# A 16-expert stage on one core: the dense expert's down products by column halves at the end, all routed rows back through DRAM and PSUM, fifteen weight slots, a new order of places

## The reference

```
h2 = rms_norm(x, g)
for e in range(16):                      # combine: two of 16 weights per token are not zero
    he = silu(h2 @ w_gate[e]) * (h2 @ w_up[e])       # 1024 -> 512
    out = out + combine[..., e] * (he @ w_down[e])   # 512 -> 1024
x = x + out
x = x + sigmoid(x @ w_ple_gate) * (p @ w_ple_proj)
return rms_norm(x, final_g)
```

## Time and profile before

| | |
|---|---|
| time, median of 3 executions (lowest, highest) | 1636.68 us (1634.86, 1639.38) |
| profiled execution, its own time | 1639.89 us |
| span in its profile, granted clock of the core | 1638.1 us, 0.976 |
| PE, POOL, ACT, DVE busy over the span | 94%, 78%, 44%, 44% |
| expert stage | from about 1219 us to 1598 us of the span |

### The profile page before, as it was taken

One profiled execution on the slowest core, in us unless ns is written; L12 is line 12 of the kernel. 1 busy time (PEld: TensorE's weight loads), 2 busy tenths in 40 slices (PEclk: granted clock), 3 DMA queues, 4 the chain that ended last, 5 costly groups with the idle time before them and its releaser, 6 DMA issues.

```text
span 1638.1 us, 22007 instructions
## 1 busy us (share of the span) xinstructions
PE 1537.1 (94%) x7044; PEld 1167.6 (71%) x7044; DVE 712.8 (44%) x1316; ACT 720.8 (44%) x887; POOL 1270.2 (78%) x1513
## 2 busy tenths in 40 slices
PE   7999999999999989899999989999999898899966
PEld 5777877788877868688788867878775465476625
DVE  3986844301037968834101067174555221212225
ACT  4544543544446554444444435546332223245423
POOL 7997898999999996869999988977663335368823
PEclk9999999999999999999999999999999999999987
DMA  6754454667765543535676655645365989889980
GB/s 220 219 167 121 136 154 142 208 212 222 214 200 168 151 145 116 154 109 167 215 217 207 190 175 155 200 140 165 116 222 213 378 291 349 334 301 341 383 329 26
DMA packets 95429, 334.62 MB, mean 204 GB/s; under 512 B 11136, under 2 KB 15760, under 8 KB 94256
## 3 DMA queue, kind: packets, MB, share of 16 engines
q1 hardware_dynamic: 90752, 314.34, 58.5%
q10 hardware_dynamic: 3440, 14.93, 2.6%
q0 software_dynamic: 1152, 4.19, 0.7%
HBM read 323.17 MB, written 21.78 MB: 211 GB/s over the span
## 4 chain that ended last, share of the span: by engine, by line
POOL 52%; PE 26%; issue 15%; DMA 3%; DVE 2%; ACT 1%; SPq 1%; POOLq 1%; DVEq 0%; ACTq 0%
POOL w_lo L1835 52%; PE bank L684 7%; PE bank L1191 5%; PE bank L1245 4%; PE bank L1188 3%; PE bank L1211 3%; DMA arena<-in_experts 2%; PE bank L1260 1%; DMA outputs_by_expert<-xn 1%; PE bank L1284 1%; POOLq L1830 0%; DMA raw<-outputs_by_expert,tiny 0%; PE bank L713 0%; PE bank L1231 0%; PE bank L1086 0%
## 5 line engine op out<-in xcount | busy, mean ns | idle before, releaser
L1835 POOL TENSOR_TENSOR w_lo<-raw,w_hi 128x256 fp32r<-128x256 f32 x1416 | 1066.6, 792 | 140.4 <-ACT w_hi L1421 139.6
L684 PE MATMUL bank<-w_hi,hT 128*128 128x512 f32 x2240 | 714.6, 400 | 33.5 <-POOL w_lo L1835 13.4
L1421 ACT ACTIVATE w_hi<-raw 128x1024 fp32r<-128x1024 f32 x356 | 377.1, 1059 | 523.9 <-DMA raw<-in_stream 261.2
L684 PEld LDWEIGHTS bank<-w_hi,hT 128*128 128x128 f32 x2240 | 415.8, 191 | 136.7 <-POOL w_lo L1835 21.0
L684 PE MATMUL bank<-w_lo,hT 128*128 128x512 f32 x1120 | 441.5, 394 | 0.0
L1842 POOL TENSOR_TENSOR w_lo<-arena,w_hi 128x1024 fp32r<-128x1024 f32 x80 | 189.5, 2386 | 155.2 <-ACT w_hi L1421 154.8
L684 PEld LDWEIGHTS bank<-w_lo,hT 128*128 128x128 f32 x1120 | 213.2, 190 | 47.0
L1421 ACT ACTIVATE w_hi<-arena 128x1024 fp32r<-128x1024 f32 x80 | 84.3, 1056 | 104.1 <-PE bank L1191 40.7
L995 PE MATMUL bank<-w_hi,mixT 128*128 128x512 f32 x352 | 111.7, 399 | 5.4 <-DVE mixT L2254 5.2
L684 PE MATMUL bank<-w_hi,mixT 128*128 128x512 f32 x288 | 91.5, 399 | 3.9 <-POOL w_lo L1835 2.5
L2246 DVE SCALAR_TENSOR_TENSOR arena<-bank,tiny,arena 128x256 f32<-128x256 f32 x44 | 21.1, 484 | 158.6 <-ACT arena L1577 143.7
(11 more groups left out here) (389 smaller groups left out, 1901.1 us busy)
## 6 DMA issues: line engine op xcount, KB each, us to landing
raw<-in_stream SPq DMA_DIRECT2D x356, 512.0 KB, 3.6
arena<-in_experts SPq DMA_DIRECT2D x192, 512.0 KB, 7.2
rows_by_expert<-in_blank ACTq DMA_DIRECT2D x56, 128.0 KB, 3.2
arena<-in_stream SPq DMA_DIRECT2D x10, 512.0 KB, 12.2
gates<-rows_by_expert SPq DMA_DIRECT2D x3, 1024.0 KB, 7.3
outputs_by_expert<-xn SPq DMA_DIRECT2D x3, 1024.0 KB, 7.9
bias_skewed<-bias_windows SPq DMA_DIRECT2D x4, 512.0 KB, 5.2
outputs_by_expert<-in_blank ACTq DMA_DIRECT2D x4, 512.0 KB, 4.5
```

Source lines behind the costliest of these rows:

```text
L684: mm = pe.matmul(LIN[t][:, :], lhs[:, a, k0 + k, t * P:(t + 1) * P], w[:, k, :], start=(k0 + k == 0 and n == 0), stop=(k0 + k == nk - 1 an ...
L1421: act.activation(w_hi[:, s, :], src, ACT.Copy).then_inc(s_hi, 1)
L1835: part = nc.gpsimd.tensor_tensor(w_lo[:, i, c], raw[:, i, c], w_hi[:, i, c].bitcast(F32), ALU.subtract)
```

## The change

1. `RANKS` becomes (0, 13, 12, 1, 11, 10, 2, 9, 8, 3, 4, 5, 6, 7, 14): the wide place of each group of three comes first. Places 9 to 14 stay.
2. Fifteen slots: twelve in `arena` and the three buffers of `raw`, which the earlier part has done with.
3. The dense expert's four down quarters are no longer split and move from the start of the stage to its end, after the second projection quarter, in the order (g, n) = (0,0), (1,0), (0,1), (1,1). Its hidden values wait in `dense_he`.
4. The last place is stored (by ACT's queue) and gathered like the others; the spread, its matrix and the second set of addresses go.
5. Rows come back by column halves: first half of x first, and s_x is counted after each half.
6. ACT's program: in a paired place no `ahead` stands among the row splits, `needed` makes only the high parts of the place before, and `ahead` in `gated` reaches two quarters on.

```diff
-DEPTH = 12
+ARENA_SLOTS = 12
+DEPTH = ARENA_SLOTS + RING
-RANKS = (13, 12, 0, 11, 10, 1, 9, 8, 2, 3, 4, 5, 6, 7, 14)
+RANKS = (0, 13, 12, 1, 11, 10, 2, 9, 8, 3, 4, 5, 6, 7, 14)
+DENSE_DOWN = ((0, 0), (1, 0), (0, 1), (1, 1))
...
-    order = [("gu", -1, g, j) for g in range(2) for j in range(4)] + [("dn", -1, 0, n) for n in range(2)]
+    order = [("gu", -1, g, j) for g in range(2) for j in range(4)]
...
-    order += [("proj", 0)] + [("dn", POSITIONS - 1, g, n) for g, n in down_parts(POSITIONS - 1)] + [("proj", 1)]
+    order += [("proj", 0)] + [("dn", POSITIONS - 1, g, n) for g, n in down_parts(POSITIONS - 1)]
+    order += [("proj", 1)] + [("dn", -1, g, n) for g, n in DENSE_DOWN]
...
+                elif s >= ARENA_SLOTS:
+                    sp.wait_ge(s_hi, FRONT_Q)
+                    sp.wait_ge(s_lo, FRONT_Q)
...
+            def dense_down(g, n):
+
+                pe.wait_ge(s_td, ready[-1, g])
+                if (g, n) == DENSE_DOWN[0]:
+                    pe.wait_ge(s_flush, POSITIONS - 1)
+                elif g == 0:
+                    pe.wait_ge(s_flush, POSITIONS)
+                w = whole_quarter(down_at(-1, g, n))
+                for t in range(TT):
+                    for k in range(QK):
+                        mm = pe.matmul(AB[2 * t + n][:, :], dense_he[:, g, k, t * P:(t + 1) * P], w[:, k, :],
+                                       start=(g == 0 and k == 0), stop=(g == 1 and k == QK - 1), skip_group_check=True)
+                mm.then_inc(s_whole, 1)
...
-                rows_turned(0, 0)
                 pe.wait_ge(s_ad, ab.back(0))
-                expert_down(-1, 0, 0)
-                rows_turned(0, 1)
-                expert_down(-1, 0, 1)
-                rows_turned(0, 2)
-                rows_turned(0, 3)
+                for i in range(4):
+                    rows_turned(0, i)
...
-                last_spread()
+                for g, n in DENSE_DOWN:
+                    dense_down(g, n)
...
+            def needed(s):
+
+                for _ in range(split_before(s + 1) - hi.n):
+                    high()
...
-                ahead(last)
+                ahead(last, 2 if paired(p) else 6)
...
+                    if paired(p):
+                        hidden_split(p - 1)
+                        if p > 0 and not paired(p - 1):
+                            needed(down_at(p - 1, 1, 1))
+                        rows_split(p + 1, 0)
+                        rows_split(p + 1, 1)
                         rows_split(p + 1, 2)
                         rows_split(p + 1, 3)
                         gated(p, 1)
                         continue
...
+                        p, at = POSITIONS - 1, first_row(POSITIONS - 1)
+                        act.wait_ge(s_ycopy, POSITIONS)
+                        for h in range(2):
+                            act.dma_start(y_rows[at:at + rows_of(p), 512 * h:512 * h + 512],
+                                          staged(p)[64 * h:64 * h + rows_of(p), 0, 0:512]).then_inc(s_ystore[p % 2], 16)
+                ahead(GATE_AT - 1)
+                for i in range(4 * TT):
+                    h, c, t = i // 4, i // 2 % 2, i % 2
+                    if h == 0:
+                        act.wait_ge(s_back[c * TT + t], 16)
+                    act.wait_ge(s_added, max(1, i))
+                    w = tiny[:, 906 + 2 * c + t:907 + 2 * c + t]
+                    act.activation(AB[2 * (i % 2)][:, :], back[c * TT + t][:, h * 512:(h + 1) * 512], ACT.Copy,
+                                   scale=w).then_inc(s_weighed, 1)
...
+            def rows_back(h):
+
+                for i in range(4 * h, 4 * h + 4):
+                    t = i % 2
+                    dve.wait_ge(s_weighed, i + 1)
+                    v = x[:, t, h * 512:(h + 1) * 512]
+                    dve.tensor_tensor(v, AB[2 * t][:, :], v, ALU.add).then_inc(s_added, 1)
+                    dve.wait_ge(s_added, i + 2)
...
+                outputs_read(POSITIONS - 1)
+                dense_outputs(0)
+                dve.memset(tc(1006), 0.0).then_inc(s_added, 1)
+                rows_back(0)
+                dve.memset(tc(1006), 0.0).then_inc(s_x, 1)
+                rows_back(1)
+                dense_outputs(1)
+                dve.memset(tc(1006), 0.0).then_inc(s_x, 1)
```

More of the change, by code:

```diff
@@ L167, in is_whole @@
         return p < 0 or paired(p) or (tiles_of(p) == 1 and q[3] % 2 == 1)
-    return kind == "proj" or (kind == "dn" and paired(p))
+    return kind == "proj" or (kind == "dn" and (p < 0 or paired(p)))
 WHOLE = frozenset(s for s, q in enumerate(ORDER) if is_whole(q))
@@ L418, in program @@
         xf = [v[:].rearrange("p s w -> p (s w)")[:, 0:4 * P].rearrange("p (k t) -> p k t", k=4) for v in (wexp, prob)]
-        back = [raw[:, 0, :], raw[:, 1, :], raw[:, 2, :], logits[:].rearrange("p h w -> p (h w)")[:, 0:D]]
+        back = [gates[:, 1, t, :] for t in range(TT)] + [logits[:].rearrange("p h w -> p (h w)")[:, 2 * t * D:(2 * t + 1) * D] for t in range(TT)]
         order = tiny[:, 208:224].bitcast(mybir.dt.int32)
@@ L1730, in hidden_split @@
             def hidden_split(p):
-                if paired(p):
+                if p < 0 or paired(p):
                     tr.up()
@@ L1784, in experts_act @@
                         continue
+                    ahead(gate_up_at(p, 0, 0))
+                    hidden_split(p - 1)
+                    gated(p, 0)
+                    rows_split(p + 1, 0)
+                    ahead(down_at(p - 1, 1, 1) if p > 0 else gate_up_at(p, 0, 3))
+                    rows_split(p + 1, 1)
                     ahead(gate_up_at(p, 1, 0))
@@ L1793, in experts_act @@
                 for n in range(2):
-                    ahead(PROJ_AT[n])
                     act.wait_ge(s_lin, lin.up())
@@ L2517, in rows_rest, with dense_outputs @@
                                   e[:, 0, k:k + 2, 0:n].bitcast(F32), ALU.subtract).then_inc(s_td, 1)
+            def dense_outputs(n):
+                dve.wait_ge(s_whole, whole_before(down_at(-1, 1, n) + 1))
+                for t in range(TT):
+                    v = x[:, t, n * 512:(n + 1) * 512]
+                    own(dve.scalar_tensor_tensor(v, AB[2 * t + n][:, :], tc(292, t), v, ALU.mult, ALU.add))
+            def rows_back(h):
[5 more added lines that the diff above has]
+                    dve.wait_ge(s_added, i + 2)
             def outputs_read(p):
+                if p < 0:
+                    return
                 if paired(p):
@@ L2545, in outputs_read @@
                 dve.memset(tc(1007), 0.0).then_inc(s_flush, 1)
-            def last_weights():
-                for t in range(TT):
-                    dve.tensor_scalar(last_by_token[:, t, :], row_tab, last_rel[:, t:t + 1], w1[:, t, :], ALU.is_equal, ALU.mult)
-                    own(dve.tensor_scalar(last_part, row_tab, last_rel[:, TT + t:TT + t + 1], w2[:, t, :], ALU.is_equal, ALU.mult))
-                    i = dve.tensor_tensor(last_by_token[:, t, :], last_by_token[:, t, :], last_part, ALU.add)
-                    if t == 0:
-                        own(i)
-                i.then_inc(s_lastw, 1)
             def experts_dve():
```

142 lines of the change are left out of this document (37 added, 105 removed).

## The result

The kernel with the change takes 1623.42 us (median of 10 executions, 1615.94 to 1632.38). The kernel before took 1636.38 us on the same chip (median of 10, 1632.01 to 1644.47). The ratio is 0.9915, with a 95% interval of 0.9888 to 0.9942: 0.6 to 1.1% faster. The forecast was 1614 us, with a range of 1606 to 1630, so the time lies in the range, 9 us above the forecast.

The account below looks back on a forecast made before the run. PE and the DMA engines were taken as nearly used up by turns, with PE pausing at three holes and the end; 1639.9 profiled less 23.1 gave 1616.8, the median 3.2 lower, so 1614 us, range 1606 to 1630.

Parts of the forecast that it names:

- Dense products removed (10.9) and hidden at the end: Expert stage: two dense down blocks of 5.47 us leave PE's path, 10.9 us; at the end the gathers hide them.
- The three holes (16.6) and their slow restarts (8): PE's pauses where a wide place follows a paired one vanish with ACT's new order: 16.6 us, plus 8 us of restarts.
- The opening (7.9 and 2.5): Start of the routed places: PE waits for a wide place's rows, adding 7.9 us, and restarts slowly, adding 2.5.
- Two waits for `w_lo` (4.2): At wide places 3 and 6, behind paired ones, PE waits 2.1 us each for the first low part: 4.2 us added.
- Local shortage (1.5): Before the end of the routed places, weight loads fall short locally: 1.5 us added, between 0 and 12.
- The rival that loads are too slow: Stretches of paired places: SP's in-order waits use up the three-slot margin, costing 12 us instead of 1.5: 1624.5 us; chance 0.17.
- T': End of the last place's down products in the changed kernel, forecast at 1557.6 us against 1577.0 before.
- S: Time for the last place's store on ACT's queue to land at the stage's end, taken as 6 us.
- the late store: Rival at the stage's end: the store takes 11.4 us like SP's stores and the clock gain is lost: 1622 us; chance 0.17.
- The restart (T' + 20.1): Behind the last place, the first half of x is ready and PE restarts 20.1 us after T', at 1577.7 us.
- The other four steps and `dense_outputs(1)` pass behind PE's first transposes and quarter: At the stage's end, the remaining row steps and dense additions, about 4.5 us, are hidden behind PE's work on x.
- I expect the full clock: PE's restart on x: after a pause of only 2.7 us the first quarter runs at full clock, saving 2.4 us.

Follow-up runs that it names:

- Experiment 9: Changed kernel with only the first of two contraction steps in the dense down products, half of them left out: 1624.34 us, ratio 0.9925.
- experiment 1: Kernel before with only the new order on ACT in paired places (rows first, high parts only as needed): 1623.53 us, ratio 0.9909.
- experiment 2: Changed kernel with the old order on ACT in paired places, all else of the change kept: 1624.32 us, ratio 0.9905.
- Experiment 10: Changed kernel with two high parts instead of three ahead of the dense gate, in both places that ask for them: 1615.91 us, ratio 0.9884.
- Experiment 7: Changed kernel with the first high part of a following wide place made between the row copies: 1620.14 us, ratio 0.9877.
- Experiment 12: Changed kernel with the last place's two stores issued by SP behind its last gate load instead of by ACT: 1627.51 us, ratio 0.9937.
- Experiment 6: Changed kernel with DVE's last two dense additions moved from behind all eight weighted additions to behind the first: 1624.77 us, ratio 0.9894.
- experiment 4: Changed kernel with the old order of places, a paired place first: 1622.07 us, ratio 0.9896.
- experiment 5: Changed kernel with an edit meant to drop one high part ahead of the dense gate, which left every engine's instructions the same: 1629.22 us, ratio 0.9933.

## Why the prediction held, step by step

- **Dense products removed (10.9) and hidden at the end.** Right as far as tested. Experiment 9 takes 6.9 of their 13.9 us away at the end, and the stage stays within 0.5 us. The 10.9 us that they took ahead of T were not measured by a run of their own.
- **The three holes (16.6) and their slow restarts (8).** Right in the cause, but not in the share of the parts. The prediction gave the holes to the order and used the slots as its margin. The order alone takes the pauses from 16.6 us to 8.7 (experiment 1), but the rest of the change without the order removes as much (experiment 2).
- **The opening (7.9 and 2.5).** PE paused 0.97 + 5.54 us; its transposes took 3.03 us instead of the 1.8 counted and its first quarter 3.58 instead of 2.76. That is 6.5 and 2.0. So the opening was 1.9 us cheaper than the 10.4 counted. Experiment 10 shows the third high part as the cause of most of it, 6.1 us.
- **Two waits for `w_lo` (4.2).** 2.25 us each, as worked out. What was left out is the quarter behind them: after the first it took 4.61 us instead of 2.76, at the lower clock, after the second 3.04, 2.1 us in all. Experiment 7 gets 4.8 of the 6.6 back.
- **Local shortage (1.5).** Pauses of 0.34, 0.68 and 1.44; only the last is a wait for a load. The rival that loads are too slow, at 12 us, fits the kernel with twelve slots in size: 9.3 us longer. Its mechanism is only partly seen there: at the wide places PE does not wait for loads itself but 3.5 to 3.6 us for low parts, whose high part had waited 1.4 to 3.1 us for its load.
- **T'.** It was predicted 19.4 us earlier and came 18.9 earlier within the stage. That this is so near is in part luck: the opening came 1.9 us cheaper, while the waits for low parts with what follows them came 2.4 and the shortage 1.0 dearer. A wait of PE ahead of the opening that the sum did not have fell from 1.65 to 0.80 us.
- **The store.** S = 6 was expected, 5.7 measured. In the changed kernel the store of the place before it, issued by SP at 1543.79, landed after 14.39 us, at the same moment, so that S could not have been much shorter with profit. Experiment 12 gives the late store: S = 12.7, stage 4.7 us longer, where 5.4 were computed for S = 11.4. At this size and load the first of the two rules cited holds (the Trainium skill, DMA: Bandwidth & Descriptors, Queues, rings and completion order); by the second, from the section Issuing engines are not separate DMA queues, moving the issue would have changed nothing but issue time.
- **The restart (T' + 20.1).** 21.5. The first gather is issued 0.5 us later than computed; the four land 1.2 to 2.1 us apart, the last after 8.09 us, where 7.4 was taken.
- **The step that failed** is "The other four steps and `dense_outputs(1)` pass behind PE's first transposes and quarter", and with it "I expect the full clock". DVE does them before the rest part of x, the first product comes 5.4 us behind the restart instead of 2.7, and its quarter takes 4.38 us where 2.8 was expected. PE had paused 4.16 us ahead of the restart, not 2.7, and paused 3.43 more behind its transposes. Cost: 2.7 + 1.6 us. Experiment 6 removes 1.6 of the 2.7 by order alone. Even in it the granted clock is not the full one behind the restart: 0.55 over the first quarter, against 0.66 in the changed kernel and 0.55 before.

The new order of places is not needed: experiment 4 is 2.9 us shorter in the stage with the old one. And the lower end of the forecast's own range is worked out as 8 us below it, while its three terms (3.5, 1.5 and 2.1) make 7.1.

Together the stage and what follows gained 16.9 us, where 23.1 were worked out: 0.5 + 1.4 + 2.7 + 1.6 account for the difference. The forecast stood against a profiled execution of 1639.9; the medians differ by 13.0 us, which agrees with 16.9 within the interval (9.5 to 18.3 us). The gain was thus forecast too high, 22.7 us between medians against 13.0, and the range, with its 16 us above the forecast, had room for that.

## What to carry to other kernels

When an in-order engine waits early for a load that is needed late, either move the instruction behind the urgent ones or deepen the buffer. Gains from edits against the same wait don't add: here the order alone gave 13.2 of the 16.0 us, so test such edits apart before adding a third. After moving work behind a new critical path, list for each engine what stands between the release and the next thing that is needed, DVE's bookkeeping additions included. Where a program's other parts vary by several us from run to run, measure the changed stage between two instructions of its own.

## What the runs showed of the hardware

A tiny operation can take ten us. In the kernel before, DVE's addition of 128 by 8 elements (L2273) took 9.51 us. POOL ran twenty low parts back to back meanwhile, which ended at 958.46 us, and the addition ended at 958.50. PE then paused 5.20 us, ahead of the expert stage:

```profile
944.61 13.85 POOL L1835 TENSOR_TENSOR w_lo<-raw,w_hi 128x256 fp32r<-128x256 f32 x20
948.99 9.51 DVE L2273 TENSOR_TENSOR small<-small 128x8 f32<-128x8 f32 x1
...
959.15 1.22 PE L995 MATMUL bank<-w_hi,mixT 128*128 128x512 f32 x2 [5.20 <-DVE mixT L2254]
```

Its two calls together took 13.9 us there, and in the changed kernel 4.8; in experiments 6 and 9, which don't touch it, 13.7 and 19.2:

```profile
L2275 DVE TENSOR_TENSOR small<-small 128x8 f32<-128x8 f32 x2 | 19.2, 9586 | 0.0
```

These two also reached the counts latest (1243.05 and 1247.62 us, against 1226.50). But the operation does not settle the start of the stage: in experiments 2, 5 and 7 its two calls took under 1 us, and the counts came at 1233.6 to 1233.9 us, as in the kernel before (1233.65). That POOL's work holds the operation up was not tested.

The granted clock behind a pause of PE is not the same each time. In the changed kernel it was 0.64 in the 4.7 us behind the first pause of 2.25 us, whose twelve products took 4.61 us, and 1.00 behind the second pause of the same length, whose twelve took 3.04:

```profile
1317.50:1322.20 4.70, 4.64 (x15) 3.67 (x15) 0.00 (x0) 0.00 (x0) 4.67 (x3) 0.64 1.02 405
1381.30:1384.40 3.10, 3.06 (x15) 2.50 (x15) 0.00 (x0) 0.00 (x0) 3.10 (x2) 1.00 1.03 410
```

In experiments 5, 6, 9, 10 and 12 the same two pauses went the same way, 4.6 us for the twelve products behind the first and 3.0 behind the second. What sets the two apart is not shown, but such a restart can't be counted at one price.
